# Three split products for retention outputs and states, norm factors on quarters of the tokens, constants loaded in two pieces

## The chip, the cores and the metric

The kernel runs on one core of a Trainium2 chip. The metric is the device time of one execution in microseconds (us); the program is timed several times and the median counts.

## What is computed

One layer of a hybrid decoder on 512 prompt tokens and 32 sample tokens (8 sequences of 4), T = 544 columns in all, with 1024 channels. A norm and a modulation give h; h is projected to queries, keys, values and gates of four retention heads and to a recurrent branch; both branches are gated, mixed and projected, and a gated feed-forward network (hidden size 2816) follows. All of it is fp32. The lines that the change touches:

```python
def rmsnorm(x, w):
    y = xf * lax.rsqrt(jnp.mean(xf * xf, axis=-1, keepdims=True) + RMS_EPS)
...
scores = jnp.einsum('bihd,bjhd->bhij', q, k) * decay[None]
intra = jnp.einsum('bhij,bjhe->bihe', scores, v)
...
s_new = ... + jnp.einsum('bjhd,bjhe->bhde', k * k_dec[None, :, :, None], v)
...
mixed = (ga * branch_ret + gb * branch_rnn) @ p['w_out']
x = x + g1 * rmsnorm(mixed, p['norm_post_mix'])
h2 = rmsnorm(x, p['norm_pre_ffn']) * (1 + sc2) + sh2
ff = (jax.nn.silu(fg) * fu) @ p['w_ffn_out']
x = x + g2 * rmsnorm(ff, p['norm_post_ffn'])
```

## The kernel before

Activations are kept as [128 channels, channel block, 544 tokens]. Most products are **split products**: a weight slab w is turned by ScalarE into w_hi (rounded to the format fp32r) and by VectorE into w_lo = w - w_hi, the activation likewise, and TensorE adds up hi*hi, hi*lo and lo*hi, each a pass over two halves of 272 columns. Weight slabs (128x1024) arrive through two buffers, are split two slabs ahead of their use (`AHEAD`), and TensorE waits for `lo_ready`. Other products are **plain fp32 products**: the retention scores (`score`, L1131), the retention outputs (`outputs`, L1148), the final states (`final_state`, L1159), transposes, and all sums over channels, which are products with a block of ones. The profile has two records for one plain fp32 product and one for a split pass or a transpose.

There is no scheduler: each engine's program is one list, written out by hand, and executed in order; semaphores order the engines. The order of a retention head is that of `retention_units`: after the projection of each tile come units such as `tv0` to `tv3` (transposes of the values), `tk` (transposes of the keys), `sc` (scores), `o01` and `o23` (outputs, four tiles of 128 channels), `fs` (final state), and `b0` to `b7` (the eight sample states). For the heads 1 to 3 the norm of the head before runs in between: `normalise` on VectorE begins behind the second value tile with a reciprocal over 544 columns. Small results go through three PSUM banks in turn (4, 5, 6); a bank is taken again only when its reader has freed it.

In a head, `v_tok` and `k_tok` (values and keys by token, keys scaled with the decay) are copied out of PSUM by ScalarE, and `decay_scores` on VectorE writes the masked scores `pm`. Outputs are, for each tile, four products with 512, 384, 256 and 128 columns; the final state is, for each of two row blocks, four products with 512 columns.

A norm's factor is found so: VectorE adds up squares in `rsn` (or TensorE sums eight squares itself, `add_squares`), TensorE multiplies by ones so that every partition holds the sum of each token, ScalarE takes the root, and VectorE the reciprocal, both of all columns of the part. After the output projection these steps alternate with the work of the first tiles of the feed-forward network: `post` 0 and 1 are the two halves of the norm behind the projection, `pre2` 0 and 1 the halves of the norm ahead of the network, and `post2` 0 and 1 the parts of 352 and 192 columns of the last norm. `add_normed` uses the `post` factors, `second_input` the `pre2` factors; `h_lo` of `second_input` is what TensorE waits for.

SyncE issues the loads. At the start they are, in this order: all constants `con`, the first of four parts of x, all vectors `vec`, the other three parts of x, and 16 slabs of 512 KB of the modulation's weights (`ada_raw`) with one weight slab in their midst. The lines of the norm's total and of the reciprocal:

```python
def total_part(key, cols, value):
    pe.wait_ge(norm_summed, value)
    dst, full = take_bank(key)
    nc.tensor.matmul(dst[:, 0:cols.stop - cols.start], ccol("ones"), rsn[:, cols], start=True,
                     stop=True).then_inc(full, 1)
...
def one_over(key, half):
    wait_freed(dve, (key, half))
    r = rsn[:, cols_of(half)]
    do(V.reciprocal(r, r))
```

## Time and profile before

| | |
|---|---|
| three runs | 1383.84, 1384.9, 1386.7 us; median 1384.9 us |
| the profiled execution | 1381.28 us, its span 1379.5 us |
| TensorE busy | 1341.7 us, 97% of the span |
| VectorE busy | 800.0 us, 58% |
| ScalarE busy | 564.0 us, 41% |
| GpSimd busy | 213.4 us, 15% |
| mean granted clock of TensorE | 0.992 |

The span is what the profiler's records cover; the execution's own time is 1.8 us longer. The medians are of other executions than the profiled one, and the profiled one was 3.6 us below their median. Busy is the union of an engine's records, and a TensorE that is busy all the time is not thereby at its best rate.

### The profile page before, as it was taken

How to read it: one execution, taken by the hardware profiler on the slowest of the kernel's cores; microseconds unless marked ns; L12 is line 12 of the kernel's file. 1: busy time of each engine (PE TensorE's matmuls, PEld its weight loads, DVE VectorE, ACT ScalarE, POOL GpSimd, SP SyncE). 2: the span in 40 equal slices, each digit the busy share in tenths (PEclk: the TensorE clock that was granted, in tenths of full speed). 3: DMA queues.
4: the chain of work that ended last, by engine and by line, in shares of the span. 5: the costliest groups of instructions: out<-in, count | busy, mean ns of one | idle time of the engine just before them, and what ended most of it. 6: DMA issues, size and time to landing. Idle time of an engine off the chain costs nothing.

```text
span 1379.5 us, 24175 instructions
## 1 busy us (share of the span) xinstructions
PE 1341.7 (97%) x10110; PEld 1246.6 (90%) x10110; DVE 800.0 (58%) x1111; ACT 564.0 (41%) x830; POOL 213.4 (15%) x324
## 2 busy tenths in 40 slices
PE   6999999999999999999999999999899999999996
PEld 3999999888997998799879988999789999999996
DVE  4568888522252684267337624884887888852224
ACT  4667778121322321242224123335555666543221
POOL 1122231000123122302320222000011121100001
PEclk9999999999999999999999999999999999999998
DMA  9522122682525344424442453226054766743323
GB/s 372 184 62 77 62 91 75 247 318 88 192 69 190 116 144 137 164 85 138 156 158 77 132 174 123 77 84 257 1 164 117 185 168 169 176 132 107 89 85 65
DMA packets 61339, 189.87 MB, mean 138 GB/s; under 512 B 6576, under 2 KB 9776, under 8 KB 60848
## 3 DMA queue, kind: packets, MB, share of 16 engines
q1 hardware_dynamic: 44592, 141.80, 30.3%
q0 software_dynamic: 15488, 44.44, 12.5%
q10 hardware_dynamic: 1152, 2.10, 0.4%
q8 instruction: 80, 1.31, 0.4%
q14 instruction: 27, 0.22, 0.0%
HBM read 164.76 MB, written 23.55 MB: 137 GB/s over the span
## 4 chain that ended last, share of the span: by engine, by line
PE 86%; DVE 7%; ACT 3%; issue 2%; DMA 2%; SPq 1%; POOL 0%; DVEq 0%; ACTq 0%; POOLq 0%
PE ps L898 55%; PE ps L1300 14%; PE ps L907 5%; PE ps L1148 3%; PE ps L1159 2%; PE ps L950 1%; PE ps L1131 1%; PE ps L1191 1%; DMA ada_raw<-in_w_ada 1%; PE ps L1177 1%; PE ps L1034 1%; SPq L812 1%; DVE w_lo L1804 1%; PE ps L1088 1%; ACT w_hi L1383 1%
## 5 line engine op out<-in xcount | busy, mean ns | idle before, releaser
L898 PE MATMUL ps<-h_hi,w_hi 128*128 128x272 f32 x1520 | 321.0, 292 | 4.3 <-DVE w_lo L1804 3.8
L898 PE MATMUL ps<-h_hi,w_lo 128*128 128x272 f32 x1520 | 314.6, 288 | 0.0
L898 PE MATMUL ps<-h_lo,w_hi 128*128 128x272 f32 x1520 | 313.5, 288 | 0.0
L1804 DVE TENSOR_TENSOR w_lo<-raw,w_hi 128x1024 fp32r<-128x1024 f32 (+2 forms) x154 | 182.3, 1188 | 213.6 <-ACT w_hi L1383 211.8
L1383 ACT ACTIVATE w_hi<-raw 128x1024 fp32r<-128x1024 f32 (+2 forms) x154 | 157.8, 1025 | 248.1 <-PE ps L898 148.1
L898 PEld LDWEIGHTS ps<-h_hi,w_hi 128*128 128x128 f32 x1520 | 240.3, 188 | 15.1 <-issue 8.2
L898 PEld LDWEIGHTS ps<-h_lo,w_hi 128*128 128x128 f32 x1520 | 238.8, 188 | 0.0
L898 PEld LDWEIGHTS ps<-h_hi,w_lo 128*128 128x128 f32 x1520 | 237.5, 189 | 0.0
L2082 DVE SCALAR_TENSOR_TENSOR state<-state,ps 128x512 f32<-128x512 f32 x64 | 41.1, 684 | 108.1 <-PE ps L1191 107.8
L2486 POOL DMA_DIRECT2D s_raw<-in_w_fin x18 | 15.6, 865 | 325.7 <-DMA s_raw<-in_w_fin 325.7
L898 PE MATMUL ps<-a_hi,w_hi 128*128 128x272 f32 x308 | 63.8, 288 | 0.2 <-DVE w_lo L1804 0.2
L898 PE MATMUL ps<-a_hi,w_lo 128*128 128x272 f32 x308 | 63.8, 288 | 0.0
L898 PE MATMUL ps<-a_lo,w_hi 128*128 128x272 f32 x308 | 63.5, 288 | 0.0
L1300 PE MATMUL ps<-h_hi,w_hi 128*128 128x272 f32 x216 | 62.3, 288 | 0.0
L1300 PE MATMUL ps<-h_lo,w_hi 128*128 128x272 f32 x216 | 62.2, 288 | 0.0
L1300 PE MATMUL ps<-x_lo,w_hi 128*128 128x272 f32 x216 | 62.2, 288 | 0.0
L1300 PE MATMUL ps<-x_hi,w_lo 128*128 128x272 f32 x216 | 62.1, 288 | 0.0
L1300 PE MATMUL ps<-x_hi,w_hi 128*128 128x272 f32 x216 | 62.1, 287 | 0.0
L1300 PE MATMUL ps<-h_hi,w_lo 128*128 128x272 f32 x216 | 61.9, 287 | 0.0
L898 PE MATMUL ps<-r_hi,w_hi 128*128 128x272 f32 x256 | 53.6, 290 | 0.0
L898 PE MATMUL ps<-r_hi,w_lo 128*128 128x272 f32 x256 | 53.0, 288 | 0.0
L898 PE MATMUL ps<-r_lo,w_hi 128*128 128x272 f32 x256 | 52.8, 288 | 0.0
(298 smaller groups left out, 2694.6 us busy)
## 6 DMA issues: line engine op xcount, KB each, us to landing
raw<-in_w_head SPq DMA_DIRECT2D x48, 512.0 KB, 3.8
state<-in_state POOLq DMA_DIRECT2D x32, 512.0 KB, 4.6
out_rs<-state POOLq DMA_DIRECT2D x32, 512.0 KB, 4.1
raw<-in_w_rnn SPq DMA_DIRECT2D x24, 512.0 KB, 3.6
ada_more<-in_w_ada SPq DMA_DIRECT2D x23, 512.0 KB, 7.9
raw<-in_w_fin SPq DMA_DIRECT2D x20, 512.0 KB, 5.3
s_raw<-in_w_fin SPq DMA_DIRECT2D x36, 256.0 KB, 5.6
s_raw<-in_w_fin POOLq DMA_DIRECT2D x36, 256.0 KB, 5.1
```

The lines of the kernel that those rows point to most:

```text
L812: sp.dma_start(ada_raw[:, n, :], w["w_ada"][n // KD, n % KD]).then_inc(ada_in[n], 16)
L898: mm = nc.tensor.matmul(dst[:, half, :], a, b[:, half * HALF:(half + 1) * HALF], start=first and j == 0, stop=last and j == 2)
L907: mm = nc.tensor.matmul(dst, a, b[:, cols], start=first and j == 0, stop=last and j == 2)
L950: mm = nc.tensor.matmul(ps[g * ROWS:(g + 1) * ROWS, bank, 0:ADA_COLS], c_rows[:, k, :], slab[:, g * ADA_COLS:(g + 1) * ADA_COLS], start=k ...
L1034: mm = nc.tensor.matmul(dst[:, half, 0:HALF], rg_w[:, n, g, :], xc[:, n % 2, half * HALF:(half + 1) * HALF], start=True, stop=True)
L1148: mm = nc.tensor.matmul(dst[:, j * P:SEQ], v_tok[:, j, o * P:(o + 1) * P], scores(j), start=j == 0, stop=j == JT - 1, skip_group_check=True)
L1159: mm = nc.tensor.matmul(dst[:, :], k_tok[:, j, d * P:(d + 1) * P], v_tok[:, j, :], start=j == 0, stop=j == JT - 1)
L1300: mm = nc.tensor.matmul(ps[:, bank, 0:HALF], a, b, start=not add and k == 0 and j == 0, stop=k == KD // 2 - 1 and j == 2, skip_group_check ...
L1383: A(hi[:, 0:cols], src[:, 0:cols], ACT.Copy).then_inc(hi_ready, 1)
L1804: V.tensor_tensor(lo[:, 0:cols], raw_slab(i)[0][:, 0:cols], hi[:, 0:cols].bitcast(F32), ALU.subtract).then_inc(lo_ready, 1)
L2082: do(V.scalar_tensor_tensor(state[:, u % STATES, d, :], state[:, u % STATES, d, :], gamma(h) ** TS, ps[:, pl.bank[key][0], :], ALU.mult, A ...
L2486: pool.dma_start(s13_raw[:, u, 0, :], w["w_fin"][n, 1][:, BLOCK:2 * BLOCK], accum_op=ALU.add)\
```

## The change

**Retention.** Outputs and final states become split products. ScalarE writes `v_hi`, `k_hi` and, new, `pm_hi` (a copy of the scores, in the unit `sc`); VectorE writes `v_lo`, `k_lo` and `pm_lo`, and it is VectorE now that frees the banks of the transposes. Each plain product becomes three passes of the same number of columns. `r_hi` and `r_lo` now lie in the memory of `gs` and `oo`, and `pm_lo` in that of `pm`.

**Norms.** The sum over channels is made for four quarters of the part's tokens side by side, each into 32 partitions (`quarter_sums`), so that root and reciprocal work on 68, 68, 68, 68, 88 and 48 columns instead of 272 (four times), 352 and 192. TensorE then spreads the factors back over all partitions with four products (`spread_factors`), into PSUM bank 7, where VectorE reads them. TensorE waits for `inverted` (VectorE) at a place that is fixed in its list, VectorE for `spread`. The split of one early slab (`fu`, EARLY - 1) moves on VectorE from ahead of the first reciprocal to behind `second_input(0)`, and ScalarE runs a root of one element early, behind the first tile of the output projection.

**Constants.** `con` and `vec` are each cut in two; the second pieces are loaded behind the modulation's slabs, and ScalarE and GpSimd wait for them (`rest_in`).

```diff
+for _name, _n in (("b_ada", 48), ("n_pre", 8), ("lru", NR), ("c", KD * NSEQ), ("n_post", 8), ("n_pre2", 8),
+                  ("n_post2", 8), ("gn", 16), ("conv_w", NR * 4), ("conv_b", NR), ("b_a", NR), ("b_x", NR), ("b_ga", 8),
+                  ("b_gb", 8), ("h0", NR * NB), ("conv_in", NR * NB * 3)):
...
+FIRST_VEC = VEC["n_post"][0]
...
+        r_scope = ExitStack()
+        r_hi = sb(r_scope, "r_hi", [P, ET, T], F32R)
+        r_lo = sb(r_scope, "r_lo", [P, ET, T], F32R)
+        r_scope.close()
...
+        v_hi = sb(ret, "v_hi", [P, JT, DV], F32R)
+        v_lo = sb(ret, "v_lo", [P, JT, DV], F32R)
+        k_hi = sb(ret, "k_hi", [P, JT, DK], F32R)
+        k_lo = sb(ret, "k_lo", [P, JT, DK], F32R)
...
+        pm_lo = sb(pm_scope, "pm_lo", [P, sum(SEQ - j * P for j in range(JT))], F32R)
...
+        NORMS = {("post", 0): cols_of(0), ("pre2", 0): cols_of(0), ("post", 1): cols_of(1), ("pre2", 1): cols_of(1),
+                 ("post2", 0): LAST_PARTS[0], ("post2", 1): LAST_PARTS[1]}
+
+        def number(key):
+            return list(NORMS).index(key)
+
+        def quarter(key):
+            return (NORMS[key].stop - NORMS[key].start) // GROUPS
+
+        def quarter_roots(key):
+            return roots_of[:, number(key) % 2, 0:quarter(key)]
+
+        def one_over_of(key, cols):
+
+            at = NORMS[key].start
+            return ps[:, 7, cols.start - at:cols.stop - at]
...
+            sp.dma_start(con[:, 0:FIRST_CON], w["con"][:, 0:FIRST_CON]).then_inc(con_in, 16)
             load_x(0)
-            sp.dma_start(vec[:], w["vec"]).then_inc(vec_in, 16)
+            sp.dma_start(vec[:, 0:FIRST_VEC], w["vec"][:, 0:FIRST_VEC]).then_inc(vec_in, 16)
...
                 sp.dma_start(ada_raw[:, n, :], w["w_ada"][n // KD, n % KD]).then_inc(ada_in[n], 16)
+            load_to(pl.slab[("gr", 0, "w", 0)])
+            sp.dma_start(vec[:, FIRST_VEC:], w["vec"][:, FIRST_VEC:]).then_inc(rest_in, 16)
+            sp.dma_start(con[:, FIRST_CON:], w["con"][:, FIRST_CON:]).then_inc(rest_in, 16)
...
-                    mm = nc.tensor.matmul(dst[:, 0:HALF], ccol("ones"), x1_sq[:, k, :], start=k == 0, stop=k == KD - 1)
+                    mm = quarter_sums(dst, x1_sq[:, k, :], HALF // GROUPS, k == 0, k == KD - 1)
                 if k == KD - 1:
                     mm.then_inc(full, 1)

-            def total_part(key, cols, value):
+            def quarter_sums(dst, x, n, first, last):
+
+                for g in range(GROUPS):
+                    mm = nc.tensor.matmul(dst[g * ROWS:(g + 1) * ROWS, 0:n], ccol("ones", 0, ROWS), x[:, g * n:(g + 1) * n],
+                                          start=first, stop=last, skip_group_check=True)
+                return mm
+
+            def total_part(key, value):

                 pe.wait_ge(norm_summed, value)
                 dst, full = take_bank(key)
-                nc.tensor.matmul(dst[:, 0:cols.stop - cols.start], ccol("ones"), rsn[:, cols], start=True,
-                                 stop=True).then_inc(full, 1)
+                quarter_sums(dst, rsn[:, NORMS[key]], quarter(key), True, True).then_inc(full, 1)
+
+            def spread_factors(key):
+
+                pe.wait_ge(inverted, number(key) + 1)
+                n = quarter(key)
+                for g in range(GROUPS):
+                    mm = nc.tensor.matmul(ps[:, 7, g * n:(g + 1) * n], ccol("ident", g * ROWS, 1).to_broadcast([P, P]),
+                                          quarter_roots(key), start=True, stop=True, skip_group_check=True)
+                mm.then_inc(spread, 1)
...
-                    wait_freed(pe, ("sc", h, j))
+                pe.wait_ge(pm_ready, JT * (h + 1))
                 for o in range(ET):
                     wait_freed(pe, ("tv", h, o))
                 for o in tiles:
                     dst, full = take_bank(("o", h, o))
                     for j in range(JT):
-                        mm = nc.tensor.matmul(dst[:, j * P:SEQ], v_tok[:, j, o * P:(o + 1) * P],
-                                              scores(j), start=j == 0, stop=j == JT - 1,
-                                              skip_group_check=True)
+                        for i, (v, s) in enumerate(((v_hi, pm_hi), (v_hi, pm_lo), (v_lo, pm_hi))):
+                            mm = nc.tensor.matmul(dst[:, j * P:SEQ], v[:, j, o * P:(o + 1) * P], scores(s, j),
+                                                  start=j == 0 and i == 0, stop=j == JT - 1 and i == 2,
+                                                  skip_group_check=True)
                     mm.then_inc(full, 1)
...
-                        mm = nc.tensor.matmul(dst[:, :], k_tok[:, j, d * P:(d + 1) * P], v_tok[:, j, :],
-                                              start=j == 0, stop=j == JT - 1)
+                        for i, (k, v) in enumerate(((k_hi, v_hi), (k_hi, v_lo), (k_lo, v_hi))):
+                            mm = nc.tensor.matmul(dst[:, :], k[:, j, d * P:(d + 1) * P], v[:, j, :],
+                                                  start=j == 0 and i == 0, stop=j == JT - 1 and i == 2)
                     mm.then_inc(full, 1)
...
+                        total_part(("post", 0), 1)
+                    if i == len(HELD) and k == KD - 1:
+                        spread_factors(("post", 0))
                     mm = half_step(key, k)
                 mm.then_inc(multiplied, 1)
             add_squares(0, range(KD))
-            total_part(("post", 1), cols_of(1), 2)
+            total_part(("post", 1), 2)
+            spread_factors(("pre2", 0))
...
                             add_squares(1, range(0, KD - 2))
                         if (half, n, k) == (0, EARLY - 1, 3):
                             add_squares(1, range(KD - 2, KD))
+                        if (half, n, k) == (0, 1, 1):
+                            spread_factors(("post", 1))
+                        if (half, n, k) == (0, EARLY - 1, 5):
+                            spread_factors(("pre2", 1))
...
-                            total_part(("post2", 0), LAST_PARTS[0], 3)
+                            total_part(("post2", 0), 3)
+                        if half and (i, j) == (0, 7):
+                            spread_factors(("post2", 0))
...
-            nc.tensor.matmul(dst, ccol("ones"), rsn[:, cols], start=True, stop=False)
+            quarter_sums(dst, rsn[:, cols], quarter(("post2", 1)), True, False)
             pe.wait_ge(sq_ready, SQUARES)
-            nc.tensor.matmul(dst, ccol("ones"), sqn[:, (KD - 1) % 2, cols], start=False, stop=True).then_inc(full, 1)
+            quarter_sums(dst, sqn[:, (KD - 1) % 2, cols], quarter(("post2", 1)), False, True).then_inc(full, 1)
+            spread_factors(("post2", 1))
...
+            def roots_of_part(key):
+                wait_full(act, key)
+                do(A(quarter_roots(key), ps[:, pl.bank[key][0], 0:quarter(key)], ACT.Sqrt, bias=eps_rms[:, 0:1],
+                     scale=1.0 / D), *freed(key), wait=False)
...
-                        do(A(k_tok[:, 2 * half, :], spare(("tk", h, half))[:, 0:DK], ACT.Copy,
-                             scale=ccol("kdec", 2 * half * H + h, 1)), wait=False)
-                        turned(("tk", h, half), k_tok[:, 2 * half + 1, :], spare(("tk", h, half))[:, DK:2 * DK],
-                               scale=ccol("kdec", (2 * half + 1) * H + h, 1))
+                        for j in (2 * half, 2 * half + 1):
+                            at = j % 2 * DK
+                            do(A(k_hi[:, j, :], spare(("tk", h, half))[:, at:at + DK], ACT.Copy,
+                                 scale=ccol("kdec", j * H + h, 1)), k_hi_ready, wait=False)
...
+                    wait_full(act, ("tv", h, e))
+                    do(A(v_hi[:, :, e * P:(e + 1) * P], spare(("tv", h, e)).rearrange("p (j c) -> p j c", j=JT), ACT.Copy),
+                       v_hi_ready, wait=False)
+                elif name == "sc":
+                    for j in range(JT):
+                        wait_freed(act, ("sc", h, j))
+                        do(A(scores(pm_hi, j), scores(pm, j), ACT.Copy), pm_hi_ready, wait=False)
...
+                if m == 0:
+                    do(A(sqn[:, 1, 0:1], eps_rms[:, 0:1], ACT.Sqrt))
...
+                for j in range(JT):
+                    dve.wait_ge(pm_hi_ready, JT * h + j + 1)
+                    do(V.tensor_tensor(scores(pm_lo, j), scores(pm, j), scores(pm_hi, j).bitcast(F32), ALU.subtract),
+                       pm_ready, wait=False)
+
+            def lo_of_values(h, e):
+                key, at = ("tv", h, e), slice(e * P, (e + 1) * P)
+                dve.wait_ge(v_hi_ready, ET * h + e + 1)
+                do(V.tensor_tensor(v_lo[:, :, at], ps[:, pl.bank[key][0], :].rearrange("p (j c) -> p j c", j=JT),
+                                   v_hi[:, :, at].bitcast(F32), ALU.subtract), *freed(key), wait=False)
+
+            def lo_of_keys(h):
+                for j in range(JT):
+                    key, at = ("tk", h, j // 2), j % 2 * DK
+                    dve.wait_ge(k_hi_ready, JT * h + 2 * (j // 2) + 2)
+                    do(V.scalar_tensor_tensor(k_lo[:, j, :], ps[:, pl.bank[key][0], at:at + DK],
+                                              ccol("kdec", j * H + h, 1), k_hi[:, j, :].bitcast(F32), ALU.mult,
+                                              ALU.subtract), *(freed(key) if j % 2 else (None, None)), wait=False)

             def split_sample_values(h):

                     for u in after.get((name, i), ()):
                         if u == "sc":
                             decay_scores(h)
+                        elif u == "tk":
+                            lo_of_keys(h)
+                        elif u[0] == "t" and u != "tvs":
+                            lo_of_values(h, int(u[2]))
...
+            def one_over(*key):
+                wait_freed(dve, key)
+                r = quarter_roots(key)
+                do(V.reciprocal(r, r), inverted)
+
+            def wait_spread(*key):
+                dve.wait_ge(spread, number(key) + 1)

             def add_normed(half, k, signal):
-                y, x, r = (t[:, prompt_of(half)] for t in (mo[:, k, :], xr_[:, k, :], rsn))
-                do(V.tensor_tensor(y, y, r, ALU.mult))
+                y, x = (t[:, prompt_of(half)] for t in (mo[:, k, :], xr_[:, k, :]))
+                do(V.tensor_tensor(y, y, one_over_of(("post", half), prompt_of(half)), ALU.mult))
                 do(V.tensor_tensor(x, x, y, ALU.add), signal, wait=False)
...
                 add_held(0, m)
-            split_to(pl.slab[("fu", EARLY - 1, "w", 0)])
             dve.wait_ge(xres_in, 16)
             dve.wait_ge(mo_ready, 1)
             one_over("post", 0)
+            wait_spread("post", 0)
             x1 = iter(range(KD))
             for m, n in zip(HELD, (4, 2, 2)):
                 for _ in range(n):
                     add_normed(0, next(x1), x1_ready)
                 add_held(1, m)
             one_over("pre2", 0)
+            wait_spread("pre2", 0)
             second_input(0)
+            split_to(pl.slab[("fu", EARLY - 1, "w", 0)])
             one_over("post", 1)
             wait_took(dve, pl.half_tile[("wo", KD - 1, 1)][0])
-            samples_normed(gate1)
+            do(V.tensor_tensor(all_samples(mo), all_samples(mo), for_samples(gate1), ALU.mult))
+            wait_spread("post", 1)
+            samples_normed()
             for k in range(KD):
                 add_normed(1, k, x1_ready)
```

How the lists change, at three places. First TensorE, head 1, the first output tile (`o01`): `ps<-pm,v_tok` is a product from scores and values, the number behind it its columns. Before:

```order
L898 MATMUL ps<-r_lo,w_hi 128x272 x2
L898 MATMUL ps<-r_hi,w_lo 128x272 x2
L1148 MATMUL ps<-pm,v_tok 128x512
L1148 MATMUL ps<-pm,v_tok 128x384
L1148 MATMUL ps<-pm,v_tok 128x256
L1148 MATMUL ps<-pm,v_tok 128x128
```

and now:

```order
L1200 MATMUL ps<-pm_hi,v_hi 128x512
L1200 MATMUL ps<-pm_lo,v_hi 128x512
L1200 MATMUL ps<-pm_hi,v_lo 128x512
L1200 MATMUL ps<-pm_hi,v_hi 128x384
L1200 MATMUL ps<-pm_lo,v_hi 128x384
L1200 MATMUL ps<-pm_hi,v_lo 128x384
L1200 MATMUL ps<-pm_hi,v_hi 128x256
L1200 MATMUL ps<-pm_lo,v_hi 128x256
L1200 MATMUL ps<-pm_hi,v_lo 128x256
L1200 MATMUL ps<-pm_hi,v_hi 128x128
L1200 MATMUL ps<-pm_lo,v_hi 128x128
L1200 MATMUL ps<-pm_hi,v_lo 128x128
```

Four plain products became twelve passes of the same widths. Second, VectorE in head 1, behind the third value tile: the rotation of the keys is `work<-ps,cosin`, the norm's work `oo` and `r_hi`, `r_lo`. Before:

```order
L1804 TENSOR_TENSOR w_lo<-raw,w_hi 128x1024
L1970 TENSOR_TENSOR work<-ps,cosin 128x544
L1971 TENSOR_TENSOR work<-ps,cosin 128x544
L2021 SCALAR_TENSOR_TENSOR oo<-oo,vec,work 128x544
L2022 TENSOR_TENSOR oo<-oo,gs 128x544
L1812 CAST r_hi<-oo 128x544
L1813 TENSOR_TENSOR r_lo<-oo,r_hi 128x544
L1804 TENSOR_TENSOR w_lo<-raw,w_hi 128x1024
L1973 TENSOR_TENSOR work<-ps,cosin 128x544
L1974 TENSOR_TENSOR work<-ps,cosin 128x544
```

and now:

```order
L1879 TENSOR_TENSOR w_lo<-raw,w_hi 128x1024
L2045 TENSOR_TENSOR work<-ps,cosin 128x544
L2046 TENSOR_TENSOR work<-ps,cosin 128x544
L2152 TENSOR_TENSOR v_lo<-ps,v_hi 128x4x128
L2096 SCALAR_TENSOR_TENSOR oo<-oo,vec,work 128x544
L2097 TENSOR_TENSOR oo<-oo,gs 128x544
L1887 CAST r_hi<-oo 128x544
L1888 TENSOR_TENSOR r_lo<-oo,r_hi 128x544
L1879 TENSOR_TENSOR w_lo<-raw,w_hi 128x1024
L2048 TENSOR_TENSOR work<-ps,cosin 128x544
```

The subtraction `v_lo<-ps,v_hi` came in ahead of the second half of the keys' rotation; one more stands nine rows further up, behind the `w_lo` before. Third, TensorE where the squares of the first half are summed (`early_raw,con`) and the second half of the norm `post` (`rsn,con`). Before:

```order
L907 MATMUL ps<-h_hi,w_lo 128x272
L968 MATMUL ps<-early_raw,con 128x272 x8
L976 MATMUL ps<-rsn,con 128x272
L907 MATMUL ps<-h_hi,early_hi 128x272
L907 MATMUL ps<-h_lo,early_hi 128x272
```

and now:

```order
L944 MATMUL ps<-h_hi,w_lo 128x272
L1012 MATMUL ps<-early_raw,con 32x68 x32
L1012 MATMUL ps<-rsn,con 32x68 x4
L1027 MATMUL ps<-roots_of,con 128x68 x4
L944 MATMUL ps<-h_hi,early_hi 128x272
L944 MATMUL ps<-h_lo,early_hi 128x272
```

The eight sums became 32 products on 68 columns and 32 output partitions, and the spread of the factors of `pre2` 0 (`roots_of,con`) stands in the list ahead of the next tile.

## Rows read from the trace of the kernel before

**Rows 1.** The page's first and second part: busy time, and granted clock in 40 slices.

```profile
PE 1341.7 (97%) x10110; PEld 1246.6 (90%) x10110; DVE 800.0 (58%) x1111; ACT 564.0 (41%) x830; POOL 213.4 (15%) x324
...
PEclk9999999999999999999999999999999999999998
```

**Rows 2.** Who waited for whom: engine, line, releaser, us in total, times, longest.

```profile
PE ps L907 <- DVE h_lo L2182: 5.6, 2, 3.8
```

**Rows 3.** Busy time by stretch: PE, PEld, DVE, ACT, POOL, PEclk, DMA share, GB/s.

```profile
480.00:612.00 132.00, 131.77 (x929) 116.47 (x928) 68.08 (x87) 35.10 (x49) 31.02 (x45) 1.00 0.41 134
...
965.00:1042.00 77.00, 69.40 (x485) 65.29 (x484) 63.05 (x112) 41.54 (x81) 3.60 (x4) 0.96 0.25 74
```

**Rows 4.** The chain that ended last: start, length, engine, line, records.

```profile
538.29 4.31 PE ps L1148 x16
...
561.06 6.87 PE ps L1159 x16
568.40 6.02 PE ps L898 x48
...
1360.39 6.02 PE ps L907 x54
```

**Rows 5.** TensorE in order of time: first and last pass with 352 columns.

```profile
1347.76 0.32 PE L907 MATMUL ps<-a_hi,w_hi 128*128 128x352 f32 x1
...
1358.10 0.32 PE L907 MATMUL ps<-a_hi,w_lo 128*128 128x352 f32 x1
```

**Rows 6.** VectorE in order of time: two PSUM operations in a row, end of the keys' rotation.

```profile
524.39 1.29 DVE L2082 SCALAR_TENSOR_TENSOR state<-state,ps 128x512 f32<-128x512 f32 x2 [0.25 <-PE ps L1191]
...
629.66 0.72 DVE L1976 TENSOR_TENSOR work<-work 128x544 f32<-128x544 f32 x1
```

**Rows 7.** TensorE in order of time: four column groups at once; the keys' transposes.

```profile
19.79 0.64 PE L950 MATMUL ps<-ada_raw,c_rows 128*32 128x256 f32 x8 [0.46 <-DMA ada_raw<-in_w_ada]
...
631.14 1.03 PE L1118 MATMUL ps<-con,work 128*128 128x128 f32 x8
```

**Rows 8.** DMA issues: KB each, median us from issue to landing.

```profile
vec<-in_vec SPq DMA_DIRECT2D x1, 332.0 KB, 5.0
con<-in_con SPq DMA_DIRECT2D x1, 280.0 KB, 2.9
```

**Rows 9.** The same chain, at the start, behind the projection and at the end.

```profile
30.73 0.64 PE ps L950 x8
...
964.84 1.19 ACT L1409
966.13 0.49 ACT rsn L1409
...
968.82 1.85 DVE rsn L2158
...
978.89 0.74 PE ps L968 x2
...
980.24 1.86 DVE rsn L2158
...
983.87 14.87 PE ps L907 x96
...
1368.01 1.36 DVE rsn L2361
```

**Rows 10.** Busy time by stretch, columns as in rows 3.

```profile
28.00:30.00 2.00, 1.63 (x16) 0.41 (x16) 1.14 (x4) 0.76 (x2) 0.00 (x0) 0.50 1.03 410
984.00:986.00 2.00, 2.00 (x9) 2.00 (x10) 1.93 (x5) 1.05 (x2) 0.00 (x0) 0.50 0.00 0
```

**Rows 11.** VectorE in order of time: h_lo of the first input, a factor from SBUF and one from PSUM.

```profile
29.93 0.73 DVE L1823 TENSOR_TENSOR h_lo<-x_in,h_hi 128x544 fp32r<-128x544 f32 x1 [0.79 <-ACT h_hi L1402]
...
972.36 0.43 DVE L2162 TENSOR_TENSOR mo<-mo,rsn 128x272 f32<-128x272 f32 x1
...
997.29 0.43 DVE L2190 TENSOR_TENSOR a_tmp<-a_tmp,ps 128x272 f32<-128x272 f32 x1
```

80 lines of the change are left out of this document (37 added, 43 removed).

## The prediction

> **What bounds the kernel now.** I read the page's busy shares first: TensorE is at work for 1341.7 of 1379.5 us, at the full granted clock in all but the last of the 40 slices to within a tenth [rows 1]. The list of waits says that it hardly waits for an engine: the largest such entry is 5.6 us in all, for the activation's low part [rows 2]. In the stretch of head 2 (480 to 612) it has work for 131.77 of 132 us, VectorE for 68.08, ScalarE for 35.10 [rows 3]. So in retention a microsecond less on TensorE is a microsecond less in the end, unless a new wait arises. The only places where TensorE is not the limit lie at the start, where loads come at 410 GB/s and its clock is granted at 0.50, the lower of the two levels (1.2 of 2.4 GHz) [rows 10]; behind the output projection, where it is busy for 69.40 of 77 us and VectorE for 63.05 [rows 3]; and at the very end, where a reciprocal stands on the chain [rows 9].
>
> **Retention: passes for plain products.** What is removed: one output tile costs 4.31 / 2 = 2.155 us, one row block of a state 6.87 us for eight records of two blocks, that is 16 records, so 3.435 us a block and 0.859 us a product of 512 columns [rows 4]. What comes in are three passes of each width. A pass with 272 columns takes 6.02 / 48 = 0.1254 us [rows 4]; one with 352, (1358.10 - 1347.76) / 65 = 0.1591 us (66 passes from first to last) [rows 5]. A straight line through them gives 0.42 ns a column, so 0.226 us for 512, 0.172 for 384, 0.119 for 256. With 192 columns a pass costs 6.02 / 54 = 0.1115 us, more than the line's 0.092 [rows 4]; I take that as a floor, so 128 columns cost 0.111.
>
> - An output tile: 3 x (0.226 + 0.172 + 0.119 + 0.111) = 1.886 us against 2.155. Sixteen tiles: -4.3 us.
> - A state block: 12 x 0.226 = 2.717 us against 3.435. Eight blocks: -5.7 us.
>
> Together 62.0 us become 51.9, -10.0. The bounds: if a pass could not go under 0.159 us at any width below 352 the outputs alone would lose the gain (3 x (0.226 + 0.172 + 0.159 + 0.159) = 2.15), leaving -5.7; if all passes cost 5% less than the line, -12.6.
>
> The Trainium skill, "TensorE: Matmul & The Clock Gate", section "Back-to-back issue gap", gives about 131 ns as the sustained spacing of matmuls with 512 columns and 81 ns for 128. By that rule (an estimate) a state block would cost 1.6 us and the whole gain would be near 29 us instead of 10. This trace has 159 ns at 352 columns already, so it speaks against the rule.
>
> **Retention: the new work of the other engines.** ScalarE copies four blocks of scores per head; VectorE does four `v_lo`, four `k_lo` and four `pm_lo`. Their nearest row is a pair of VectorE operations on 512 columns out of PSUM: 1.29 / 2 = 0.64 us [rows 6]. The eight that are not `v_lo` hold 128 to 512 columns, on average half of that, so VectorE gets some 4 x 0.64 + 8 x 0.45 = 6.3 us a head. In a head it is idle for 132 - 68 = 64 us, ScalarE for 97 [rows 3]; the cover is there on average, and costs nothing where it is.
>
> At one place it is not. In heads 1 to 3 VectorE works without a break from the reciprocal of the previous head's norm to the end of the keys' rotation, which ends at 629.66 + 0.72 = 630.38 [rows 6], and TensorE begins the keys' transposes, which wait for it, at 631.14 [rows 7]. The slack is 0.76 us. The second place of the order shows two `v_lo` put in ahead of the rotation: 2 x 0.64 = 1.29 us. So TensorE waits 0.5 us, with its handover 0.6, three times: **+1.8 us**. The bounds are 0, if VectorE's operations in front are shortened by earlier starts, and the full 6.3 a head (a rival). The banks of the value transposes are now freed by VectorE, later than ScalarE did; head 0 has no norm in front, so no stall there.
>
> **Constants.** 262 of the 332 KB of `vec` and 152 of the 280 KB of `con` go behind the modulation's slabs [rows 8]; the pieces follow from the column counts of the two tables. The loads run at 410 GB/s there [rows 10], so the slabs come 414 / 410 = 1.0 us earlier. On the chain stands the slab's product at 30.73 [rows 9]; `h_lo` ends at 29.93 + 0.73 = 30.66, just ahead of it [rows 11], and gains only the 0.4 us that `con` gives. But most of the modulation's products wait for slabs anyway, as does the first of them in [rows 7]. -0.4 to -1.0; I take **-1.0**. The second pieces, 414 KB, land beside stretches at a DMA share of 0.41 and less [rows 3]: nothing.
>
> **The norm behind the projection.** Before, on the chain: ScalarE's table load 1.19, the root, VectorE ready only at 968.82 (it splits an early slab first), reciprocal 1.85, so 970.67 [rows 9]. Now the table load is done ahead, the root covers a quarter of the columns (0.49 becomes 0.25), the split is gone. The reciprocal: 1.36 us for 192 columns and 1.85 for 272 [rows 9], so 6.1 ns a column, and 0.60 for 68. Starting from the same 966.13: 966.13 + 0.25 + 0.60 = 966.98. Then TensorE spreads the factors: four products, eight records, of 68 columns; at the floor of 0.111 each 0.9 us, four at once in column groups 0.64 for eight records in [rows 7] though of 256 columns; I take 0.5 to 0.9. So 967.5 to 967.9, **2.8 us earlier**. At the second reciprocal the chain goes from the squares' end at 978.89 + 0.74 to 980.24 + 1.86 = 982.10 [rows 9]; now 0.25 + 0.60 + 0.9 takes the place of 2.5, another -0.8: `second_input` can start 3.6 us earlier. TensorE's 14.87 us for 96 passes at 983.87 hold 12.0 us of work at full speed; the rest goes to the lower clock: it is at 0.50 in 984 to 986 [rows 9, 10], after TensorE, done with the squares at 979.63, had next to nothing to do until 983.87. Half of the other 2.9 us I put down to the clock; if the shorter idle stretch spares that fall, 1.4 us more come back.
>
> Not all of 3.6 to 5.0 lasts. Three spreads now stand at fixed places in TensorE's list, and VectorE must still do the second half of `add_normed` and of the input, 63 of 77 us busy [rows 3]. A late factor now stops TensorE, not VectorE alone. I take **-4.5**, with 0 and -6 as bounds. The moved split of the early slab falls behind `second_input(0)`; it is done long before its tile (the last early one) is up.
>
> The Trainium skill, "VectorE: DVE Perf Modes", the section on the TRN2 errata, gives VectorE a fixed part of 120 cycles from PSUM and 58 from SBUF. By it (an estimate) some 30 operations with factors from bank 7 would cost 65 ns more each, +2 us. This case's rows have 0.43 us for 272 columns with the factor in SBUF, and 0.43 with an operand in PSUM [rows 11]; the sum goes by them, at nothing.
>
> **The end.** Last part: reciprocal of 48 columns instead of 192, 1.36 [rows 9] minus 0.88; the root 0.2 less; against that a spread and two handovers between engines, 0.5 to 1.3, and a spread of 88 columns (0.9) in TensorE's list during the last tile, less the sum of 352 columns, now a quarter (-0.4). **0**, plus or minus 0.6.
>
> **Sum.** -10.0 + 1.8 - 1.0 - 4.5 + 0 = -13.7. The profiled execution took 1381.28 us, so 1367.6; that one lay 3.6 us under the median, so on the median of 1384.9 some 1371.2. I say 1371.
>
> **The rivals.**
>
> *VectorE becomes the bound in the late heads.* If the norm, the rotation and the split chain run back to back over the whole head, all 6.3 us a head come onto the path instead of 0.6: 3 x 5.7 = +17, or, if half of it finds the idle stretches, +9: 1380. For it: the slack at the keys is only 0.76 us. Against it: 64 us idle in each head [rows 3]. 0.12.
>
> *The middle does not pay.* TensorE waits in order at the spreads, or its clock falls all the same, and the gain is 0 to 1 instead of 4.5: about 1375. For it: four handovers between engines where there were two, and TensorE busy for 69 of 77 us [rows 3]. 0.16.
>
> *The line bends above 352 columns* (the slower side). Two passes' worth for 512 columns, 0.43 us as in a plain product's record, would make outputs and states 104 instead of 62 us: 1423. It decides from 27% over my 51.9 us (65.7): then outputs and states are 3.7 above before and the sum is 0. Against: 272 to 352 rises by the clock's pace of one column a cycle (0.42 ns at 2.4 GHz). 0.04.
>
> *The passes come cheaper than the line* (the rule above): wide passes at 131 ns, gain 29 us in retention: 1352. 0.02.
>
> *The split doesn't change the rate,* as the loads of weights bind (PEld is busy for 116.47 of 132 us [rows 3]) and three passes cost as much as the product: outputs and states 0, others as above: 1381. 0.04.
>
> **How the numbers follow.** The forecast case has 0.62; its own range is 1366 to 1376 (bounds of the middle, of the passes' 5%, of the start). The low end of the range lies at 1363, for a middle at its best, no stall and passes 5% under the line; the high end at 1379, which takes in the failed middle and most of the VectorE case. Outside it are the bend, the cheap passes, the unchanged rate and part of the VectorE case, under 2 in 10. A change under 0.2% (2.8 us) is about what a measurement of this kernel can't tell from none: slower takes the bend, 0.04; same some of the unchanged rate and of VectorE, 0.04; faster the rest, 0.92.
>
> **What would show it.** Each step is right if: a head's output pair falls from 4.31 to about 3.77 us, a state pair from 6.87 to 5.43; the keys' transposes in heads 1 to 3 have an idle time ahead of them, released by VectorE's rotation, of about 0.6 us; the product at 30.73 stands at 29.7; `second_input` of the first half starts at about 3.6 us less, besides what retention moved; the window behind it has fewer slices at clock 0.50. Wrong if: idle time of TensorE at scores or outputs is released by `pm_lo`, at spreads by the reciprocal for more than 1 us in all, or the twelve passes of a tile cost over 2.1 us.

## The result

Four runs of the changed kernel took 1373.99 to 1375.14 us, median 1374.95; four of the kernel before 1383.84 to 1386.7, median 1384.61. The ratio is 0.9929, 95% interval 0.9916 to 0.9941: 9.7 us faster (8.2 to 11.6). The prediction was 1371.0 in a range of 1363 to 1379. The direction and the mechanism held; the gain came out 4 us smaller than forecast. The profiled execution took 1375.0 us with a span of 1373.2 us.

The page of the changed kernel, its first and second part as in [rows 1]:

```profile
PE 1336.7 (97%) x10380; PEld 1263.0 (92%) x10380; DVE 815.3 (59%) x1159; ACT 569.0 (41%) x847; POOL 206.9 (15%) x324
...
PEclk8999999999999999999999999999999999999998
```

TensorE is still the bound and is busy for only 5.0 us less. Its chain of work, start and length, against [rows 4 and 9]:

```profile
30.88 1.08 PE ps L987 x8
...
540.53 3.80 PE ps L1200 x24
...
562.35 5.46 PE ps L1212 x24
568.28 6.02 PE ps L935 x48
...
978.56 9.34 PE ps L944 x54
...
1357.17 4.71 PE ps L944 x42
1363.61 1.10 PE ps L1027 x8
```

A pair of output tiles went from 4.31 to 3.80 us, a head's state from 6.87 to 5.46. By these rows eight pairs and four states save 8 x 0.51 + 4 x 1.41 = 9.7 us; 10.0 were forecast. But the slab's product that stood at 30.73 and was to come to 29.7 stands at 30.88 and takes 1.08 us instead of 0.64, and new waits are in the list of waits (in all, times, longest):

```profile
PE ps L987 <- DMA ada_raw<-in_w_ada: 4.6, 7, 2.1
...
PE ps L944 <- DVE h_lo L2285: 2.7, 2, 1.8
PE ps L1027 <- DVE roots_of L2255: 2.0, 2, 1.0
...
PE ps L1160 <- POOL k L2563: 1.1, 3, 0.4
...
PE ps L1170 <- DVE work L2051: 0.9, 3, 0.3
```

Three waits on the keys' rotation (`work`), as forecast, and three on GpSimd's `k`, which were not. `roots_of` is the reciprocal for which the spreads wait. In order of time in head 2, TensorE and then GpSimd:

```profile
631.49 1.09 PE L1170 MATMUL ps<-con,work 128*128 128x128 f32 x8 [0.32 <-DVE work L2051]
632.96 0.42 PE L1160 MATMUL ps<-con,k 128*96 128x128 f32 x2 [0.37 <-POOL k L2563]
...
631.50 1.40 POOL L2563 COPY k<-work 128x192 f32<-128x192 f32 x1 [18.27 <-DVE work L2051]
```

The reader sees one late operation cost twice. The keys' transposes start when VectorE has rotated; at that moment GpSimd only starts its copy of the sample keys, 1.40 us long, and the transposes of these copies stand right behind in TensorE's list. Before, the rotation was 0.76 us ahead of the transposes and the copy (630.44 to 631.85 there) ended before TensorE asked for it.

The stretches of [rows 3] and two at the second input:

```profile
480.00:612.00 132.00, 131.09 (x963) 120.92 (x962) 74.94 (x100) 36.86 (x54) 28.90 (x45) 1.00 0.40 134
965.00:1042.00 77.00, 70.82 (x645) 68.40 (x645) 61.58 (x117) 41.13 (x83) 3.57 (x4) 0.96 0.25 77
...
978.00:980.00 2.00, 1.44 (x6) 1.47 (x7) 1.93 (x5) 0.89 (x3) 0.00 (x0) 0.50 0.00 0
980.00:982.00 2.00, 2.00 (x11) 2.00 (x10) 1.93 (x5) 1.15 (x3) 0.00 (x0) 0.50 0.00 0
```

VectorE got 6.9 us more work per head (6.3 were worked out), and nearly all of it lay beside TensorE. The granted clock of TensorE (third column from the end) still falls to 0.50 behind the second reciprocal. On VectorE the five steps of the norm behind the projection and their waits:

```profile
964.11 0.58 DVE L2255 RECIPROCAL roots_of<-roots_of 128x68 f32<-128x68 f32 x1 [1.29 <-ACT roots_of L1477]
965.96 0.44 DVE L2262 TENSOR_TENSOR mo<-mo,ps 128x272 f32<-128x272 f32 x1 [1.27 <-PE ps L1027]
...
976.83 0.91 DVE L2278 SCALAR_TENSOR_TENSOR mo<-x_res,scale,ps 128x272 f32<-128x272 f32 x2 [1.27 <-PE ps L1027]
...
988.85 0.42 DVE L2270 TENSOR_TENSOR mo<-mo,ps 128x256 f32<-128x256 f32 x1 [1.79 <-PE ps L1027]
...
1002.03 0.84 DVE L2278 SCALAR_TENSOR_TENSOR mo<-x_res,scale,ps 128x240 f32<-128x240 f32 x2 [1.60 <-PE ps L1027]
```

The reciprocal is 0.58 us instead of 1.85, 1.27 less, and each time VectorE then waits 1.27 to 1.79 us for TensorE's spread. What is left is what lies ahead of the reciprocal.

### The profile page after: what moved, and what is told of

It reads as the page before. It is cut to its first block, busy times and chain, and to the rows that moved or that the text cites. A ratio compares the mean times of both kernels' runs of the same rounds, so it can differ in the third digit from the quotient of the medians.

```text
span 1373.2 us, 24780 instructions
## 1 busy us (share of the span) xinstructions
PE 1336.7 (97%) x10380; PEld 1263.0 (92%) x10380; DVE 815.3 (59%) x1159; ACT 569.0 (41%) x847; POOL 206.9 (15%) x324
## 4 chain that ended last, share of the span: by engine, by line
PE 77%; issue 7%; DVE 7%; DMA 4%; ACT 3%; SPq 1%; POOL 1%; DVEq 0%; ACTq 0%; POOLq 0%
PE ps L935 49%; PE ps L1360 14%; PE ps L944 5%; PE ps L1200 2%; DMA out_rs<-state 1%; PE ps L987 1%; PE ps L1183 1%; DMA ada_raw<-in_w_ada 1%; PE ps L1212 1%; PE ps L1244 1%; PE ps L1230 1%; PE ps L1086 1%; DMA raw<-in_w_out 1%; SPq L846 1%; DVE w_lo L1879 1%
```

## The experiments

**The three parts alone, and the kernel before once more.** Each part's hunks of the diff were put into the kernel before by themselves; the fourth run is that kernel unchanged.

> Retention part alone (split outputs and states, moved r_hi/r_lo), norms and constants as before. Theory: 24 passes for an output pair cost 3.80 us (plain 4.31), for a state pair 5.46 (plain 6.87), so TensorE has 9.7 us less; at the keys' transposes of heads 1 to 3 it loses 1.1 us each, because VectorE ends the rotation later and GpSimd's copy of 1.4 us starts only then: together -6 us, ratio 0.9957. Rival: the new waits cost more than these three stalls (the full VectorE work of the late heads), then -3 us or less.

> Norm factors on quarters alone, retention and constants as before. Theory: 3.0 us behind the output projection and about 0.5 us at the end: -3.5 us, ratio 0.9975. Rival: the norm's gain rests on what retention shifted (spare), then about 0.

> Constants in two pieces alone. Theory of the prediction: slabs come 1 us earlier, -1 us, ratio 0.9993. Rival A: nothing (0), since a stretch at clock 0.50 right behind the modulation takes what the loads gave. Rival B: the split of the constants itself causes the longer stretches at clock 0.50 (30 to 35 and 41 to 45 us in the changed kernel's profile), then +2 to +3 us.

> The kernel before, unchanged, for a second trace. If its profiled execution lies near 1384.6 us instead of 1381.3, its trace shows where the 3.3 us are: theory: at the start, in stretches at clock 0.50 between 23 and 45 us, as in the changed kernel's profile. Rival: its start is like the first profile's and the 3.3 us lie somewhere else.

| | median, us | ratio to before | interval | us |
|---|---|---|---|---|
| retention alone | 1379.69 | 0.9956 | 0.9943 to 0.9968 | -6.1 |
| norms alone | 1380.97 | 0.9978 | 0.9965 to 0.9991 | -3.0 |
| constants alone | 1384.41 | 0.9998 | 0.9987 to 1.0010 | -0.3 |
| before again | 1384.59 | 0.9999 | 0.9990 to 1.0009 | 0 |

(us: the ratio times the 1384.6 us of before.) The sum is -9.4, the whole change -9.7: within the intervals, about 1.8 us to either side for each part, the parts add up. Retention and norms came near their theories (-6 and -3.5), which were written with the trace of the changed kernel at hand. For the constants the time alone does not tell -1 from 0, but it does rule out the rival of +2 to +3.

The trace of the unchanged kernel's second profile (1386.39 us) shows where my first profile had been an unusual one. The same pass, the first of the projection that follows the third tile's gates, in the first trace of before:

```profile
123.66 0.49 PE L898 MATMUL ps<-h_hi,w_hi 128*128 128x272 f32 x2 [0.28 <-DVE w_lo L1804]
```

and in the second:

```profile
127.24 0.36 PE L898 MATMUL ps<-h_hi,w_hi 128*128 128x272 f32 x1 [0.26 <-DVE w_lo L1804]
```

The granted clock (third column from the end) in the first trace of before:

```profile
30.00:33.00 3.00, 2.80 (x31) 1.29 (x24) 2.66 (x4) 2.94 (x5) 0.00 (x0) 0.92 1.03 411
41.00:44.00 3.00, 3.00 (x26) 3.00 (x25) 1.18 (x2) 2.06 (x3) 0.41 (x3) 1.00 0.33 102
```

and in the second:

```profile
30.00:33.00 3.00, 2.81 (x20) 1.12 (x17) 2.61 (x4) 2.94 (x5) 0.00 (x0) 0.50 1.02 406
41.00:44.00 3.00, 3.00 (x17) 3.00 (x18) 2.34 (x4) 2.70 (x5) 0.00 (x0) 0.65 0.61 180
```

The same program came 3.6 us later to the same instruction; the low clock (1.2 GHz) ended 4.6 us later, at 35.1 instead of 30.5, and came a second time from 41.9 us on. The profile of the changed kernel has the late start too (its first such pass stands at 126.98), the profile of before that I predicted from had the early one. Most of why the two profiled executions differ by 6.3 us and the medians by 9.7 lies there. The traces also size the constants: among the late starts this pass stands at 127.24, 126.76 and 126.58 with the constants in one piece, mean 126.9, and at 125.62 to 126.98 in seven kernels with two pieces, mean 126.1; among the early ones at 123.66 with one piece and 122.91 with two (the kernel with three edits, below). So -0.8 us, from three traces that lie 0.7 us apart and seven that lie 1.4 apart: an indication. The slab's product that stood at 30.73 stands at 31.12 in the second trace of before and at 30.16 with the constants alone, 0.96 us earlier, both in late starts; at the pass of the projection 0.53 of it is left (127.24 and 126.71).

**The stalls in the late heads.**

```diff
-NORMALISE_AFTER = [("v", 2), ("v", 3), ("k", 0)]
+NORMALISE_AFTER = [("v", 2), ("v", 3), ("k", 1)]
```

> The changed kernel, with the last of the three parts of the previous head's norm on VectorE (2.8 us) moved from ahead of the second half of the keys' rotation to behind it. Theory: the stall at the keys' transposes and at the sample keys' transposes (1.1 us in each of heads 1 to 3) goes, -3.3 us against the changed kernel's 1374.95, to 1371.6, ratio to the kernel before 0.9906. Rival: TensorE then waits as long at the queries' rotation or at the scores, which come 2.8 us later on VectorE, and the time stays at 1375.

```diff
-             ("q", 0): ["tk"]}
+             ("q", 0): ["tk"], ("q", 1): ["tks"]}
...
-                pe.wait_ge(k3_ready, h + 1)
-                turn_samples(("tks", h), k3, 2)
...
+                elif name == "tks":
+                    pe.wait_ge(k3_ready, h + 1)
+                    turn_samples(("tks", h), k3, 2)
```

> The changed kernel, with the transposes of the sample keys alone, which wait for GpSimd's copy of 1.4 us, moved one tile on (behind the second query tile). Theory: of the 1.1 us per head the second wait goes (0.37 us of idle time and the refill behind it, some 0.5 us), -1.5 us: 1373.5. Rival: the wait on GpSimd only follows from the first one and costs nothing of its own: 1375.

In the first of these the norm's last quarter is multiplied by a part of the rotated keys, which by then stand where its factors were, so it does not compute the layer and only its time is of use; the instructions and waits are the same as in a right one, and the kernel with three edits (below) keeps the factors elsewhere. Measured: 1372.06 us, ratio 0.9911 (0.9896 to 0.9926), 2.9 us under the changed kernel by the medians and 2.5 by the ratios, where 3.3 were expected; and 1374.02, ratio 0.9928 (0.9915 to 0.9940), 0.9 and 0.1 us where 1.5 were. By the times alone neither is clear of the changed kernel's 0.9916 to 0.9941. The traces are sharper. From one head's keys' transposes to the next's it is 763.39 - 631.14 = 132.25 us before and 762.49 - 631.49 = 131.00 in the changed kernel. The first experiment's, TensorE in order of time:

```profile
630.25 0.27 PE L1170 MATMUL ps<-con,work 128*128 128x128 f32 x1
...
760.13 0.27 PE L1170 MATMUL ps<-con,work 128*128 128x128 f32 x1
```

No wait stands ahead of them, and the head takes 129.88 us: 2.37 less than before, which is all that the passes save in a head (2 x 0.51 + 1.41 = 2.43). Of it the changed kernel keeps 1.25 and loses 1.12 to the stalls. In the second experiment the rows are

```profile
631.60 0.33 PE L1171 MATMUL ps<-con,work 128*128 128x128 f32 x1 [0.30 <-DVE work L2054]
...
762.30 0.33 PE L1171 MATMUL ps<-con,work 128*128 128x128 f32 x1 [0.31 <-DVE work L2054]
```

so 130.70: only 0.3 us a head came back. That is not the price of the copy, because a new wait took its place. Step by step against the first experiment's head, TensorE comes 0.47 us later to the keys' transposes in both kernels; from there to the next pass of the projection the changed kernel takes 1.65 us and the first experiment 1.01, so the second wait costs 0.64. In the second experiment this 0.64 is gone, but 14.6 us behind the keys' transposes TensorE waits for VectorE's `acc` and loses 0.3. Ahead of `acc` VectorE's split of a weight slab took 1.39 instead of 1.23 us there, with GpSimd's work on the sample keys, now later, beside it:

```profile
646.18 0.49 PE L936 MATMUL ps<-r_hi,w_hi 128*128 128x272 f32 x2 [0.24 <-DVE acc L2111]
```

So of the 1.12 us a head the late rotation costs 0.5 and the copy 0.6. In the first experiment the rival (another wait takes over) fell: the queries' rotation came 2.8 us later on VectorE and nobody waited for it. It shows one thing more. GpSimd's copy takes 1.40 us in every trace in which VectorE splits a weight slab beside it, and 0.35 here, where a part of the norm stands there instead:

```profile
627.90 0.35 POOL L2563 COPY k<-work 128x192 f32<-128x192 f32 x1 [15.45 <-DVE work L2051]
...
627.87 0.95 DVE L2096 SCALAR_TENSOR_TENSOR oo<-oo,vec,work 128x544 f32<-128x544 f32 x1
```

The second wait thus hangs on what VectorE does next, and not only on when the rotation ends.

**The spread for the second half, and the clock.**

```diff
-                        if (half, n, k) == (0, 1, 1):
+                        if (half, n, k) == (0, 1, 0):
                             spread_factors(("post", 1))
...
             second_input(0)
-            split_to(pl.slab[("fu", EARLY - 1, "w", 0)])
             one_over("post", 1)
             wait_took(dve, pl.half_tile[("wo", KD - 1, 1)][0])
             do(V.tensor_tensor(all_samples(mo), all_samples(mo), for_samples(gate1), ALU.mult))
+            split_to(pl.slab[("fu", EARLY - 1, "w", 0)])
             wait_spread("post", 1)
```

> The changed kernel, with TensorE's spread of the factors of the second half of the norm behind the projection one step earlier, and VectorE's split of the early slab behind the reciprocal instead of ahead of it. VectorE waits 1.8 us for this spread in the changed kernel's trace. Theory: the second half begins some 1.2 us earlier and the end follows: 1373.7. Rival: TensorE now waits for the reciprocal at the earlier place and loses what VectorE gains: 1375.

```diff
             total_part(("post", 1), 2)
+            claim_half(("fg", 0, 0))
+
+            def filler(n):
+                for _ in range(n):
+                    nc.tensor.matmul(out_half(("fg", 0, 0))[:, 0:2 * P], ccol("ones"), con[:, 0:2 * P], start=True, stop=True)
+            filler(2)
             spread_factors(("pre2", 0))
+            filler(3)
```

> The changed kernel, with five products more on TensorE around the spread of the factors of the first half (two ahead, three behind it; their results are overwritten), in its idle time before the second input. Theory: the granted clock stays at 1.00 between 976 and 984 us, where it was at 0.50, and the first pair of half tiles ends 1.1 us earlier: 1373.9. Rival: the clock falls all the same, or the second input's pace on VectorE (0.95 us a channel block) sets the end: 1375.

Measured 1373.67 us, ratio 0.9926 (0.9914 to 0.9939), and 1373.72, ratio 0.9927 (0.9915 to 0.9940): 1.3 and 1.2 us under the changed kernel by the medians, 0.4 and 0.3 by the ratios, neither clear by its time alone. The traces: from the start of the second input's first half to VectorE's first token product of the second half of `add_normed` (`mo<-mo,ps 128x240`) it is 989.76 - 976.83 = 12.93 us in the changed kernel, 989.54 - 977.09 = 12.45 with the earlier spread, and 988.21 - 976.26 = 11.95 with the five products. With them the clock is full throughout, the stretches of that kernel:

```profile
978.00:980.00 2.00, 2.00 (x13) 1.78 (x14) 1.93 (x5) 1.05 (x2) 0.00 (x0) 1.00 0.00 0
980.00:982.00 2.00, 2.00 (x14) 1.71 (x14) 1.93 (x5) 1.04 (x2) 0.00 (x0) 1.00 0.00 0
```

Against the changed kernel's trace this is 1.0 us with the clock kept up, as expected, and 0.5 of the expected 1.2 for the spread: there VectorE's wait only shrank from 1.79 to 1.20 us,

```profile
988.63 0.42 DVE L2270 TENSOR_TENSOR mo<-mo,ps 128x256 f32<-128x256 f32 x1 [1.20 <-PE ps L1027]
```

since TensorE, at the low clock, reached even the earlier place late. Single traces do not settle this, though. Four more kernels have this stretch as the changed one has it, and for them it is 12.14, 12.88, 12.94 and 13.32 us; the shortest is the one whose clock was at 0.50 for 3.4 us only instead of 6.8. So like has to be set against like. The longest is that of the first experiment on the stalls, and its low clock lies as in the trace with the earlier spread, from about 0.9 to 7.7 us behind the start of the second input: 13.32 against 12.45, so the spread gave 0.9. The kernel with all three edits (below) is at the full clock throughout, as the one with the five products is: 980.70 - 969.53 = 11.17 us against 11.95, so it gave 0.8 there, and VectorE no longer waits for the spread:

```profile
979.79 0.41 DVE L2280 TENSOR_TENSOR mo<-mo,ps 128x256 f32<-128x256 f32 x1
```

**Everything together, and the start.** The last norm's part in both kernels below works with its own factors (they lie in the queries' memory for the heads 1 to 3's norms).

```diff
-        rs_gn = rot[:, 0, :]
+        def rs_gn(h):
+            return q_r[:, 0, :] if h < H - 1 else rot[:, 0, :]
```

> The changed kernel with three edits: the last third of the previous head's norm behind the keys' rotation (its factors now in the queries' memory for heads 1 to 3, so that the rotation does not overwrite them), the earlier spread with the later split, and the five products that keep TensorE's clock up. Theory: 3.4 us (three stalls of 1.1) plus 1.0 (clock) plus 0.5 to 1 (spread): 1370.0, ratio to the kernel before 0.9895. Rival: the edits in the middle hide each other, 1371.

```diff
+            def fill(key, n):
+                for _ in range(n):
+                    nc.tensor.matmul(out_tile(key)[:, 0, 0:2 * P], ccol("ones"), con[:, 0:2 * P], start=True, stop=True)
...
                 first_slab(1, k)
+                if k < 5:
+                    fill(("xr", 0), 1)
...
             first_tiles("xr", (3,))
+            fill(("gr", 0), 5)
```

> The same, with ten products more on TensorE at the start (one behind each of five slabs of the modulation, five in its wait for the low part of a weight slab); their results are overwritten. Theory: the stretches at clock 0.50 from 23 to 34 and from 41 to 45 us become shorter, and 2 to 3.4 us come back: 1367. Rival: TensorE is bound by the slabs there whatever its clock, or the products themselves delay the slabs' products: no change, 1370.

> The kernel before with the same ten products at the start. Theory: its two traces differ by 3.6 us at the end of the first stage, by the clock alone; with the clock kept up the median 1384.6 falls to 1381.5 or so. Rival: 1384.6 as before.

The three edits give 1370.05 us, ratio 0.9891 (0.9877 to 0.9905), where 1370.0 was expected: the best kernel of this study, 4.9 us under the changed one (5.3 by the ratios). The rival of 1371, in which the edits hide each other, is within the interval, but the traces speak against it: the heads take 129.88 us each, and from the second input to the network's 1512 passes it is 58.35 us against 60.15 in the changed kernel, 59.65 with the spread alone and 59.15 with the products alone. With the ten products at the start it is 1369.96, 0.9897 (0.9883 to 0.9910), no different; in the kernel before they make it slower, 1386.15, 1.0012 (1.0003 to 1.0022). That theory fell. The trace shows where the gain went (kernel before with the ten products, TensorE):

```profile
23.67 1.08 PE L950 MATMUL ps<-ada_raw,c_rows 128*32 128x256 f32 x8 [1.08 <-DMA ada_raw<-in_w_ada]
24.69 1.22 PE L1017 MATMUL ps<-con 128*128 128x256 f32 x2
25.94 1.08 PE L950 MATMUL ps<-ada_raw,c_rows 128*32 128x256 f32 x8
```

The clock had fallen before the first of them. At 0.50 a slab's product takes 1.08 us and an added one 1.22, together 2.3, while slabs come every 1.28; TensorE fell behind the loads, and the first tile's first pass stands at 33.15 instead of 31.30. There is no clock of 0.50 from 41 us on, but that does not show that the five at the second place did it: the early start of before has none there either. The first pass of the projection comes at 125.47, between the two traces of before, so this trace does not show where the 1.5 us by which the median is longer come from; its execution, 1384.97 us, was 1.2 under that median. In the kernel with the three edits and the ten products the low clock lasted from 25.2 to 28.6 us only, and the pass still stands at 123.92, 1.0 us behind the 122.91 of the same kernel without them, which had the early start.

**The last norm.** The two parts of the last norm back to whole columns; roots, reciprocals and products follow suit:

```diff
-                            total_part(("post2", 0), 3)
-                        if half and (i, j) == (0, 7):
-                            spread_factors(("post2", 0))
+                            pe.wait_ge(norm_summed, 3)
+                            dst, full = take_bank(("post2", 0))
+                            nc.tensor.matmul(dst[:, 0:LAST_PARTS[0].stop], ccol("ones"), rsn[:, LAST_PARTS[0]], start=True,
+                                             stop=True).then_inc(full, 1)
```

> The changed kernel with the two parts of the last norm as before (all 352 and 192 columns), the four others on quarters. Theory: TensorE's last tile ends 0.9 us earlier without the spread, but GpSimd's stores of the first part start 1.6 us later against the end and the last store lands 1.7 us later: 1375.8. Rival: the last norm makes no difference, 1375, as the prediction had it.

Measured 1375.47 us, ratio 0.9940 (0.9928 to 0.9952), against 0.9929 for the changed kernel: slower by 0.5 us by the medians and by 1.5 by the ratios, where 0.8 was expected, and the intervals overlap, so by the time it is not shown. The traces show both halves of it. GpSimd's stores of the first part and VectorE's last operation, first with whole columns:

```profile
1358.45 4.93 POOL L2601 DMA_DIRECT2D out_y<-mo  x4 [153.42 <-DVE mo L2458]
...
1366.31 0.56 DVE L2465 TENSOR_TENSOR x_res<-x_res,mo 128x384 f32<-128x384 f32 x1
```

and in the changed kernel:

```profile
1358.81 4.93 POOL L2600 DMA_DIRECT2D out_y<-mo  x4 [152.19 <-DVE mo L2457]
...
1368.32 0.56 DVE L2464 TENSOR_TENSOR x_res<-x_res,mo 128x384 f32<-128x384 f32 x1
```

With quarters the stores of the first part start 10.1 us ahead of VectorE's end, with whole columns 8.4. The span goes on for 1373.2 - 1368.88 = 4.3 us behind VectorE with quarters and 1373.5 - 1366.87 = 6.6 without. All traces agree: 3.7 to 4.8 us in the eight kernels with quarters, 6.0 to 7.3 in the six without, mean 4.2 and 6.6. The last store takes less from its issue to its landing (last number), first with whole columns and then with quarters:

```profile
out_y<-x_res SPq DMA_DIRECT2D x1, 192.0 KB, 5.4
```

```profile
out_y<-x_res SPq DMA_DIRECT2D x1, 192.0 KB, 3.7
```

From the first pass with 352 columns to the end of the span it is 30.4 to 31.1 us in the eight and 31.7 to 33.0 in the six, means 1.5 apart. In both kernels shown here the share of the DMA engines is 1.00 or more from 1361 us to 1371, so the span ends when the stores are through and not a fixed time behind VectorE.

## Why the prediction was right, and where its sizes were off

*Retention, the passes* (-10.0): 9.7 by the rows above. The straight line from 272 and 352 columns held to 512: twelve passes of 512 columns take 5.46 / 2 = 2.73 us against the 2.717 worked out, an output tile 1.90 against 1.886. The rival in which the line bends is out. So is the one by the rule of the Trainium skill, "TensorE: Matmul & The Clock Gate", "Back-to-back issue gap": 2.73 / 12 = 228 ns for 512 columns, where the page's sustained figure is 131. The line of one column in 0.42 ns decides here.

*The stall at the keys* (+1.8): mis-sized. It is 1.12 us a head, 3.4 in all. Predicted was one wait of 0.5, with its handover 0.6 us, and that one came out at 0.5. What was missing is the second, 0.6 us: I named who waits for the rotation on TensorE but not that GpSimd's queue waits for it too, with 1.40 us of work of its own on the way to the next transposes. The idle times in the records are only 0.69 us of the 1.12; the rest is seen in the starts of the passes alone. The order of the lists had shown it; the row of GpSimd's copy was in the trace of before.

*The other new work at nothing*: right. No wait of TensorE is put down to `pm_lo`, `v_lo` or `k_lo`. The time of the heads without the stall is what the passes give, to 0.1 us, with VectorE at 75 of 132 us. The rival of VectorE as the bound in the whole head is out. (It was priced at 1380 in its milder form and still said to lie mostly within a range that ends at 1379; that was a slip.)

*The constants* (-1.0): 1.0 at the slab's product and some 0.8 at the projection by the traces, not resolved by the times. In the profiled execution of the changed kernel it can't be seen at 30.88, because one slab came 0.8 us later than the others' pace and the clock stayed low.

*The norm behind the projection* (-4.5): mis-sized, -3.0. From VectorE's last sum of the first half (964.54 before, 962.37 now) to the first `add_normed` it was 6.16 us and is 3.59, so 2.6 of the 2.8 came; to the second input 17.59 and 14.46, so 3.1 of 3.6 (17.57 to 17.59 and 14.43 to 14.46 in all traces); to the start of the network's 1512 passes (1042.17 and 1036.98) 77.63 and 74.61: 3.0. The second half of the tokens gave nothing: its two reciprocals are 1.27 us shorter each, and VectorE waits 1.79 and 1.60 us for spreads that stand at fixed places in TensorE's list. I had priced these as a risk, not a term. And the clock fell all the same, the "1.4 us more" did not come; the kernels with the five products show that about 1.0 was there to have. Before, VectorE waited for nobody at the second half and began it 11.34 to 11.35 us behind the second input in every trace; now it begins 12.14 to 13.32 us behind it, by when and how long the clock is low. TensorE, for its part, waits 2.0 us in all for the reciprocal at the spreads (1.0 here, 1.0 at the end), more than the 1 us that the prediction had named as a sign of being wrong. The rival in which the middle does not pay is out by these traces; the time of norms alone, 0.9978, holds the end as well and would not rule it out.

The section on the TRN2 errata in the Trainium skill's "VectorE: DVE Perf Modes" would by its fixed parts (an estimate) have made the factors from PSUM 65 ns dearer each. Here 272 columns take 0.44 us with the factor from PSUM (965.96), and 0.43 before with it from SBUF [rows 11]: at most 10 ns. The measurement decides.

*The end* (0): off the other way. The spread and the handovers cost 0.8 us on the chain: from the start of the last long row of passes in the chain (78 in both, 1347.92 before and 1342.52 now) to VectorE's end it is 25.55 us before and 26.36 now. But the last stores land 2.4 us sooner against VectorE's end (the means above): -1.6 together. That GpSimd's earlier stores of the first part are the reason, because they share the DMA engines with the last ones, fits the busy DMA engines and the shorter last store but was not tested apart. The prediction looked at the chain of engines, stopped at the last VectorE operation and had no term for the stores.

*The sum.* -9.7 + 3.4 - 0.8 - 3.0 - 1.6 = -11.7 by the traces; the times say -9.7, with -11.6 at the edge of their interval, and the second trace of before against the changed kernel's says 1375.0 - 1386.39 = -11.4. Of that last number 1.8 us are no gain: the second profiled execution of before lay so much above its median, the changed kernel's on it. Most of the 2 us between traces and times are in the norms (-4.6 by the traces, -3.0, with -4.8 as bound, by the time of norms alone). Beyond that I can't place them. That the total by the traces is only 2.0 us off the forecast -13.7 is in part luck: the stall and the middle came out 3.1 us worse than forecast, and the end, which was forecast at nothing, gave 1.6 back. The traces scatter by 1 to 1.6 us in head 0, where GpSimd's queue waits for stores of states, and one trace a kernel does not average that out.

## What to carry to other kernels

When a step is put ahead of an operation that has little slack, look up every queue that starts on that operation's end, not only the one with the visible wait: here a copy on a third engine more than doubled the stall, and moving 2.8 us of unhurried work behind the operation gave it all back. A factor that is worked out on fewer columns but must pass through a busy in-order engine pays only where that engine is there in time; place the spread by when its input is ready, and note that VectorE's pace there then hangs on TensorE's clock. And where the one profiled execution is off the median (3.6 us here), take a second trace before comparing stages: the two profiled executions alone show 6.3 us of a gain of 9.7.

## What was unexpected of the hardware

The same program, unchanged, ran through its first 127 us with two patterns of the granted clock, 3.6 us apart: at 0.50 from 23.7 to 30.5 us in one trace; from 24.8 to 35.1 and again from 41.9 to 45.3 in the other. Of the twelve traces without added products at the start ten have the long pattern; the first one of before and that of the best kernel have the short one. In the second trace of before and in the changed kernel's, TensorE had stood for 1.74 and 2.09 us ahead of the tenth slab's product (at 26.00 and 25.76), in the two short ones for 0.82 and 0.59 (25.62 and 23.98); but in some traces with the long pattern no wait for a slab is over 1.2 us, so what sets the pattern is open.

Work that is added to hold TensorE's clock helped where it came ahead of the fall: with the five products around the spread the clock stays at 1.00 there in three traces of three, without them it falls to 0.50 in eleven of eleven. From the second input to the network's passes that is 59.15 us, against 60.15 in the changed kernel and 59.35 to 60.52 in the four others that are the same there. At the start, where the clock was down already (2.3 us of work a slab against 1.28 between slabs), it gained nothing and made the kernel before 1.6 us slower.

A small copy on GpSimd took four times as long, 1.40 instead of 0.35 us, when VectorE split a weight slab at the same time; VectorE's own 1.23 us did not change by it.
